# Token chunks in the order 512, 512, 256 instead of 256, 512, 512 in both normalisations of both layers of a diffusion step

## The reference

```python
op, os_ = mixer(hp), mixer(hs)                      # context, latent; both end in "@ w_out"
xp = layer_norm(ALPHA * xp + g1_p * op, ln1_g[i], ln1_b[i])
xs = layer_norm(ALPHA * xs + g1_s * os_, ln1_g[i], ln1_b[i])
fp = swiglu(xp * (1.0 + sc2_p) + sh2_p, ffn_w_in[i], ffn_w_out[i])
fs = swiglu(xs * (1.0 + sc2_s) + sh2_s, ffn_w_in[i], ffn_w_out[i])
xp = layer_norm(ALPHA * xp + g2_p * fp, ln2_g[i], ln2_b[i])
xs = layer_norm(ALPHA * xs + g2_s * fs, ln2_g[i], ln2_b[i])
```

## Time and profile before

| what | value |
|---|---|
| three runs | 4127.9, 4131.18, 4132.21 us (median 4131.18) |
| the profiled execution | 4131.54 us, span 4129.8 us |
| mean PE clock that was granted | 0.945 of full speed |
| PE, DVE, ACT, POOL busy | 89%, 35%, 25%, 31% of the span |
| DMA | 376 MB, mean 91 GB/s |

### The profile page before, as it was taken

The page is one execution under the profiler, slowest core; times in us unless marked ns, Lnnn a source line. Parts: engine busy times, 40 slices in busy tenths (PEclk is TensorE's granted clock), DMA queues, the critical chain, the costliest instruction groups (busy, mean ns, idle before and its releaser), DMA issues. The chain is left out here.

```text
span 4129.8 us, 51427 instructions
## 1 busy us (share of the span) xinstructions
PE 3670.1 (89%) x19140; PEld 3084.0 (75%) x19140; DVE 1458.2 (35%) x2322; ACT 1036.4 (25%) x1496; POOL 1265.0 (31%) x812
## 2 busy tenths in 40 slices
PE   5867999857899999999997998788889999999996
PEld 1556777746778888888875877788877888888885
DVE  5433222334452433334353111566613111221116
ACT  2321111102343111111124221566625111111113
POOL 2332111343353222222244120555525222222222
PEclk9788999978999999999997999899999999999997
DMA  1452222454422222212214343766520111111111
GB/s 42 150 168 95 76 86 82 126 181 168 158 66 65 64 67 72 76 58 67 68 60 164 128 155 116 177 157 151 124 87 27 41 37 41 37 42 36 37 36 56
DMA packets 150186, 376.13 MB, mean 91 GB/s; under 512 B 16615, under 2 KB 67047, under 8 KB 147976
## 3 DMA queue, kind: packets, MB, share of 16 engines
q1 hardware_dynamic: 144136, 361.71, 28.4%
q10 hardware_dynamic: 5888, 12.06, 0.9%
HBM read 294.01 MB, written 79.69 MB: 90 GB/s over the span
## 5 line engine op out<-in xcount | busy, mean ns | idle before, releaser
L143 POOL TENSOR_TENSOR w_lo<-w_raw,w_hi 128x1024 fp32r<-128x1024 f32 (+1 forms) x241 | 580.1, 2409 | 1717.7 <-ACT w_hi L137 1717.7
L137 ACT ACTIVATE w_hi<-w_raw 128x1024 fp32r<-128x1024 f32 (+1 forms) x241 | 250.6, 1040 | 1391.7 <-PE ps_r L151 459.5
L151 PE MATMUL ps_r<-a_hi,w_hi 128*128 128x512 f32 (+1 forms) x2112 | 540.6, 359 | 27.8 <-issue 11.7
L151 PE MATMUL ps_r<-a_lo,w_hi 128*128 128x512 f32 (+1 forms) x2112 | 536.5, 357 | 0.0
L151 PE MATMUL ps_r<-a_hi,w_lo 128*128 128x512 f32 (+1 forms) x2112 | 536.2, 357 | 0.0
L151 PEld LDWEIGHTS ps_r<-a_hi,w_hi 128*128 128x128 f32 x2112 | 352.0, 189 | 99.8 <-issue 18.3
L151 PEld LDWEIGHTS ps_r<-a_hi,w_lo 128*128 128x128 f32 x2112 | 352.0, 189 | 62.1
L151 PEld LDWEIGHTS ps_r<-a_lo,w_hi 128*128 128x128 f32 x2112 | 352.1, 189 | 61.9 <-issue 1.0
L1498 DVE SCALAR_TENSOR_TENSOR x_t_l<-ps_r,mod,x_t_l 128x1024 f32<-128x1024 f32 x320 | 268.2, 880 | 293.0 <-PE ps_r L151 293.0
L1483 DVE TENSOR_TENSOR hid_l<-hid_l,ps_r 128x1280 f32<-128x1280 f32 x44 | 65.4, 1487 | 864.1 <-PE ps_r L151 864.1
L1333 POOL TENSOR_TENSOR hid_lo_l<-hid_l,hid_hi_l 128x1280 fp32r<-128x1280 f32 x44 | 140.5, 3194 | 520.4 <-ACT hid_hi_l L1252 520.4
(11 more groups left out here) (216 smaller groups left out, 6424.1 us busy)
## 6 DMA issues: line engine op xcount, KB each, us to landing
w_raw<-in_w_all SPq DMA_DIRECT2D x225, 512.0 KB, 3.7
ada_w_l<-in_ada_t SPq DMA_DIRECT2D x59, 512.0 KB, 3.6
ada_raw<-in_ada SPq DMA_DIRECT2D x44, 512.0 KB, 4.1
q_hl<-q_d SPq DMA_DIRECT2D x64, 320.0 KB, 5.6
v_hl<-v_d SPq DMA_DIRECT2D x128, 128.0 KB, 2.8
k_hl<-k_d SPq DMA_DIRECT2D x32, 384.0 KB, 8.5
spec<-gout SPq DMA_DIRECT2D x40, 256.0 KB, 4.0
g_spec<-spec ACTq DMA_DIRECT2D x20, 512.0 KB, 4.6
```

What stands on the lines that cost most here:

```text
L137: act.activation(wh[:, s, 0:width], raw[:, s, 0:width], ACT.Copy).then_inc(w_hi, 1)
L143: pool.tensor_tensor(wl[:, s, 0:width], raw[:, s, 0:width], wh[:, s, 0:width].bitcast(F32), ALU.subtract).then_inc(w_split, 1)
L151: last = pe.matmul(out[:, c0:c1], w[:, c % 2, blk * 128:blk * 128 + 128], x[:, c0:c1], start=start and b == 0 and term == 0, stop=stop and ...
```

## The change

`ORDER` lists the chunks by place. It was (2, 0, 1), so the 256 context tokens came first, then the two halves of the latent tokens; now it is (0, 1, 2), the context tokens last. `ends1` and `ends2` name the units that signal the end of a weight instead of a product; they are those of the last chunk in the order.

```diff
-        ORDER = (2, 0, 1)
+        ORDER = (0, 1, 2)
...
-                ends1 = {(m, 1): e0 + m + 1 for m in range(8)}
-                ends2 = {(3, 1): eq - 1, (7, 1): eq}
+                ends1 = {(m, 2): e0 + m + 1 for m in range(8)}
+                ends2 = {(3, 2): eq - 1, (7, 2): eq}
```

## The result

| | before | after |
|---|---|---|
| median of 20 runs each | 4128.67 us | 4134.97 us |
| range of the runs | 4120.33 to 4134.62 | 4128.11 to 4148.99 |
| the profiled execution (span) | 4131.54 (4129.8) | 4136.92 (4135.1) |
| mean granted clock | 0.945 | 0.943 |

The ratio of the times is 1.0018 with a 95% interval of 1.0010 to 1.0025: 7.4 us, and 4.1 to 10.3 (the two medians differ by 6.3, the means by 7.3). The forecast was 1.0026 (4142.3 against 4131.54), just above that interval; its range of 4133 to 4151 us holds the measured median and also 4131.54 + 7.4 = 4138.9. The prediction called slower only what lies above 4139.4 and gave that 0.64.

The account below looks back on a forecast made before the run. TensorE is busy 89% of the span, so only waits were counted (VectorE's chain in second normalisations). First normalisations 4.8 + 0.8 and 5.3 + 0.8, start -2.5, second normalisations 0.8 + 0.8: +10.8 on 4131.54 gives 4142.3 us, range 4133 to 4151.

Parts of the forecast that it names:

- Second statistics: First normalisation, unit (6, 2): TensorE's wait before the second chunk's statistics grows from 2.42 to 8.0 us, chain 15.4, cover 7.3.
- Last accumulate: First normalisation, before the first peeled matmul: TensorE's wait for the last accumulate grows from 1.22 to 3.0 us.
- Low parts 1.35: First normalisation, last chunk: waits for activations' low parts total 1.35 us instead of 2.13, with 8.55 us of TensorE work before.
- w_lo 2.1: First weight after the peeled matrices: TensorE waits 2.1 us for its low part, behind SiLU and the high part.
- Clock, +0.8: Each first normalisation: longer waits leave TensorE at 1.2 GHz longer, +0.8 us per stage, bounds -1.6 and +3.5.
- rival 3: First normalisations: TensorE stays at 1.2 GHz through both narrow units, second low stretch follows, 3.5 us more each; 4149 us, chance 0.16.
- Start of layer 1, -2.5: Start of layer 1's stage: 2.8 us more cover before the first accumulate shortens TensorE's 7.84 us wait, net -2.5 us.
- Second normalisation, +0.8 each: Both second normalisations: VectorE idles 3.5 us more early, 3.3 less at the tail, plus 0.6; +0.8 us each, bounds ±3.
- Rival 1: All four stages: short tail pays if the second-statistics and last-accumulate waits together grow under about 2 us; 4119 us, chance 0.05.
- Rival 2: Half hidden: the 2.1 us behind SiLU is covered and second normalisations end even; 4136 us, no measurable change, chance 0.27.

Follow-up runs that it names:

- experiment 4: Changed kernel with VectorE's normalise steps and tile 7's sum reordered in the first normalisation's tail; ratio 1.0008 to the kernel before, tails 83.49 and 83.47 us.
- experiment 8: Changed kernel with ScalarE's square of tile 7, second chunk, behind two modulations instead of four; one profile, no total: wait for second statistics 5.99 us in both layers.
- experiment 10: Kernel before with tiles 0 to 5 in the new order, VectorE's step 4 before tile 7's sum, and POOL's weight low part later; ratio 0.9984 to the kernel before.
- experiment 11: Kernel of experiment 10 with VectorE's normalise step 4 of the second chunk between tile 7's sum and squares; ratio 0.9987 to the kernel before.
- experiment 9: Changed kernel, layer 0's second normalisation: GpSimd's last two low parts wait for VectorE's third diagonal; one profile, no total: last statistics to next stage 16.49 instead of 17.68 us.
- experiment 1: Kernel before with the new chunk order in the first normalisation of both layers only, old order in the second; ratio 1.0017, +7.0 us.
- experiment 2: Kernel before with the new chunk order in the second normalisation only; ratio 1.0000.
- experiment 7: Kernel before with tiles 6 and 7 of the first normalisation going 512, 256, 512 and tiles 0 to 5 going 512, 512, 256; ratio 1.0021.
- experiment 5: Changed kernel with ScalarE making the next weight's high part before SiLU in each feed-forward's first step; ratio 1.0012 to the kernel before, tails 84.49 and 84.43 us.
- experiment 3: Kernel before with the new chunk order only in tiles 0 to 5 of the first normalisation; ratio 0.9996, both tails 81.29 us.

## Why the prediction came out as it did

The changed stages in all profiles that run them with the old or the new order and otherwise unedited (us; range, mean, count; "predicted" for a tail is its waits and the 0.8 of the clock, layer 0 first):

| stretch | old order | new order | measured | predicted |
|---|---|---|---|---|
| tail of a first normalisation | 79.64 to 81.29, 80.6 (6) | 85.23 to 85.85, 85.5 (6) | +4.9 each | +5.6 and +6.1 |
| of it PE idle | 9.5 (6) | 13.5 (6) | +4.0 | +4.8 and +5.3 |
| of it PE busy | 71.1 (6) | 72.0 (6) | +0.9 | +0.8 |
| tiles 0 to 5, layer 1 | 97.55, 95.57 | 91.61 to 94.80, 93.0 (11) | -3.6 | -2.5 |
| second normalisation, layer 0 | 79.96 to 80.79, 80.5 (6) | 80.91 to 83.41, 82.5 (6) | +2.0 | +0.8 |
| the same, layer 1, to the end | 75.54 to 78.49, 76.3 (6) | 77.29 to 78.65, 77.8 (7) | +1.5 | +0.8 |

**Second statistics, 8.0 us.** Measured 7.97 in both layers, by the chain described: from the spread of chunk 0 (3123.00) to the statistics (3138.31) it is 15.3 us with 7.3 of PE's work in it, 15.4 and 7.3 in the prediction. Experiments 4 and 8 each cut it by 2.0 us, from two sides.

**Last accumulate, 3.0 us.** 2.81 and 2.59; from the spread of chunk 1 (3146.77) to the first peeled matmul (3152.96) it is 6.2 us, 6.4 in the prediction.

**Low parts 1.35, w_lo 2.1.** Measured 0.72 and 1.87. The chain from the third spread (3172.83) to the last low part takes 9.9 us as worked out, but PE's work in front of it is 9.3 us and not 8.55 (10.0 us to the row at 3182.83, less 0.72). Waits together 13.5 instead of 14.45: this is the part of the sum that was too large.

**Clock, +0.8.** The matmuls of a tail take 0.9 us more by the means, 1.5 in each layer of the two kernels' own profiles. The size came out, its working only in part. These are the two stretches at the lower level in the changed kernel's tail of layer 1 (columns as in the earlier trace rows):

```profile
3133.29:3146.94 13.65, 8.63 (x34) 7.62 (x35) 6.94 (x16) 6.10 (x10) 6.63 (x7) 0.50 0.01 1
3153.77:3157.18 3.41, 3.41 (x10) 2.67 (x9) 1.57 (x4) 2.79 (x5) 3.16 (x4) 0.50 0.01 5
```

The first begins within the 7.97 us wait and lasts through the statistics and the rest of the narrow unit (6, 2); the second comes behind the 2.59 us wait. PE works 12.0 us at 1.2 GHz in them. In the kernel before it was 6.8 us, in two stretches of 3.42 us, behind the waits of 2.42 us and 2.54 us. By these windows, at half pace, that alone would be 2.6 us more (an estimate); why the matmul time grew by less isn't shown, so part of the hit is luck. Much of what rival 3 described did happen, then, the second low stretch included, but not its price: PE is at 2.4 GHz again for most of unit (7, 2), and the tails are 85.2 to 85.9 us where rival 3 needs over 89. The Trainium skill (TensorE: Matmul & The Clock Gate, "Loop structure matters more than you think") says that long waits between matmuls make the engine run cold; the trace agrees for the 7.97 us, and waits of 2.4 and 2.5 us had low stretches behind them too. More waiting goes with a lower mean clock, but not in proportion: 0.90 with 13.5 us of waits in a tail (new order), 0.94 to 0.98 with 9.5 (old order), and again 0.94 to 0.98 with 7 to 8 (experiments 10 and 11).

**Start of layer 1, -2.5.** The wait itself shrank by 2.47 us in every kernel with the new order there (7.84 to 5.37), the whole stretch by 3.6; the other 1.1 us are matmuls that took less time, at a mean clock of 0.93 to 0.96 instead of 0.92 and 0.95. The old order has two profiles only.

**Second normalisation, +0.8 each.** The sign was right and the size too small, above all in layer 0. DVE's idle time before the first and second statistics there was, first a row of the kernel before that the earlier trace rows lacks, then the changed kernel:

```profile
2148.29 0.17 DVE L1380 COPY st_in<-ps_x 128x8 f32<-128x8 f32 x1 [1.97 <-PE ps_x L1068]
```
```profile
2163.48 0.17 DVE L1380 COPY st_in<-ps_x 128x16 f32<-128x16 f32 x1 [3.29 <-PE ps_x L1068]
2191.03 0.17 DVE L1380 COPY st_in<-ps_x 128x16 f32<-128x16 f32 x1 [5.68 <-PE ps_x L1068]
```

So it grew by 1.3 us before the first statistics and by 1.0 before the second (4.72 in the earlier trace rows), and shrank by 2.35 before the third (6.45 to the 4.10 of experiment 9): +1.3, +0.8 and -2.4 were predicted. What was not in the sum is the collision of experiment 9, 1.2 us, and no row of before shows it, since POOL is done there when these statistics come. Without it layer 0's +2.0 would be the predicted 0.8, although the one profile with the edit is hardly shorter as a whole (82.17 us, inside the range of the others). What makes the +1.5 of layer 1 stays open; its old order alone scatters by 3 us.

**The sum.** By these means 2 x 4.9 - 3.6 + 2.0 + 1.5 = +9.7 us (tiles 0 to 5 of layer 0 come out even), near the +10.8 of the forecast; the totals say +7.4 (4.1 to 10.3), and the stage sum lies at the upper end of that. Experiments 1 and 2 together give +7.0, and there it is the second normalisations that don't show: 3.5 us by the stages, 0.0 by the total, whose interval reaches to 4.1. The code between the changed stages scatters more than that: from the second normalisation of layer 0 to the attention's end it took 779 to 790 us in 13 profiles. What hides 3 us, or whether anything does, stays open.

Rival 1 (the short tail pays) fell with the two waits, which grew by 7.0 us a stage where under 2 was its condition. Rival 2 (half hidden), 4136 us, lies nearer to the measured total than the forecast, but one half of its mechanism is wrong: the wait after SiLU that it had as covered is there with 1.87 us. Its other half, second normalisations that end even, is against the stage means, but the total of experiment 2 doesn't exclude it.

## What to carry to other kernels

The width of a chunk counts twice: as work of its own chain and as cover for its neighbour's. A wide chunk's chain wants a wide chunk's matmuls behind it, so the narrow one belongs ahead of the wide ones: of the three orders that ran, the tail took 80.6 us with it first, 85.5 with it last and 85.9 with it in the middle, where two chains lacked cover (experiment 7). For tiles 0 to 5 of layer 1 it is the other way round: a wide chunk first cut the wait at the start by 2.5 us. Before a wait is bought off with a new order of the data, look at what its chain's engines do while they wait: DVE's 2.66 us of idle time behind ACT's queue took one `normalise` step, and two such moves with an order on POOL, the narrow chunk kept first, took 4 us from a tail (80.6 to 76.7). And when one wait is taken out, write down who is late next, or about half of it comes back (experiments 4 and 5).

## What was not expected of the hardware

An operation of 128 x 4 elements on VectorE takes 0.17 us alone and 1.19 us beside GpSimd's subtraction of two SBUF tensors, and ends when that ends. Waits of 2.42 and 2.54 us in a stretch where TensorE is else busy each had 3.4 us at 1.2 GHz behind them in the kernel before, layer 1; behind like waits it was 3.4 us in all in experiment 2 and 10.2 in experiment 3. With a wait of 8.0 us the low stretches of the changed kernel held 12.0 us of matmuls instead of 6.8.
